# First block of a two-block fp32 network: V and O projections token-major, cross-attention keys and values between the hyena steps, stacked filter matmuls

## Chip, core and metric

One core of one Trainium2 chip runs the whole program in one launch. The metric is the device time of the launch in microseconds, the median of three runs. The engines are TensorE (PE: matmuls; PEld is its loading of weights), VectorE (DVE), ScalarE (ACT), GpSimd (POOL) and SyncE (SP, which issues most DMAs). Tiles have 128 partitions; on chip memory is SBUF, and matmuls write into the eight banks of PSUM, of 128x512 fp32 each.

## The reference

T = 512 tokens, D = 1024, 256 memory tokens, all fp32. `rms` is a norm over the features. Only the first block is touched, and from the second block a table of the decay's rates.

```
u = rms(x, mix_g) @ w_in                       # 1024 -> 1536 (z, g1, g2) + 1024 (q, k) + 512 v + 512 o + 16 gates
hy = conv3(u[:, :1536]);  qk = silu(conv3(u[:, 1536:2560]))
hid  = sin(fr1 * (feat @ w1 + b1)); hid = sin(fr2 * (hid @ w2 + b2))
filt = (hid @ w3) * decay                      # L x (2 orders, 2 directions, 512)
spec = rfft(concat(filt fwd, 0, flip(filt bwd[1:])))
z, g1, g2 = split(hy)
for o, gate in ((0, g1), (1, g2)):             # hyena
    z = gate * (irfft(rfft(z, 2L) * spec[o])[:L] + z * skip[o])
y_hy = group_rms(z, 8 groups)
y_ml = group_rms(sigmoid(o_pre) * (mlstm(q, k, v, gates) + mlstm of the reversed tokens), 4 heads)
h = x + concat(y_hy, y_ml) @ w_out
k_mem, v_mem = rms(mem, mem_g) @ wk, rms(mem, mem_g) @ wv
h = h + softmax(rms(h, x_g) @ wq · k_mem / 16) v_mem @ wo
h = h + square(relu(rms(h, ff_g) @ ff_w1)) @ ff_w2
out = second_block(rms(h, fin_g))              # gated convolution, RG-LRU with rate 8 * softplus(-lam), gated FFN
```

## The kernel before

Every weight comes as a strip of 128x1024 fp32 (512 KB), 302 in all, in a ring of four slots. SP loads strip n + 4 when TensorE has done strip n. ScalarE copies a strip to `w_hi`, rounded to fp32r (`high`; `ahead(n)` does strip n + 3, L882). POOL forms `w_lo = raw - w_hi` in two halves (`low`, L440). Activations are split into `XH` and `XL` in the same way, and each product is three matmuls of 128x128 by 128x512: high by high, low by high, high by low (`three`, L472 to L474). `strip` does 24 of these for one output tile of 128 features by 512 tokens. Activations are thus feature-major, [features, tokens].

Five blocks of code, one for each engine, are written out by hand, and semaphores join them: `lo_ready` (a strip's low half is there), `pe_done` (a strip is used), `evac` (a PSUM bank is read), and many of one stage alone. Each engine runs its instructions in the order of its block; nothing is scheduled by a planner.

The order of strips on TensorE, which is that of all queues:

1. 16 strips of memory's keys (8, with 256 columns) and values (8) against the normed memory `NH`, `NL`. Between them stand the matmuls of the hyena's filter: `feat @ w1`, `hid @ w2` and, at four places (`TAPS_AFTER`), four matmuls `hid @ w3` (L550), from which VectorE makes forward and backward taps, their sum and difference (`sums_and_differences`) and low halves (L1281). VectorE then squares and splits x.
2. Spectrum: 5 strips of cosines and sines against the taps, which ScalarE copies out to `Hc`, `Hs`, `HB`.
3. The norm of x (L500), then 8 strips for V and O, feature-major; VectorE scales each (L1340), TensorE transposes it (`turn`, L575), ScalarE copies it to `VX` or through a sigmoid to `TM`.
4. 8 strips for q and k with VectorE's convolution of three taps; 1 strip of gates; the first 4 of 12 strips for z, g1, g2 (32 of 96 `blocks` of one k tile each), convolved by VectorE (`z_convolved`, L1367 to L1379) and turned (`z_turn`, L575). VectorE computes the gates' cumulative sums between them.
5. The walk: 32 mLSTM steps (4 heads, 2 directions, 4 chunks of 128). In a step TensorE does q·k (L662) and its share of the other 64 blocks of z; `row` (L636) broadcasts a gate row every four steps. VectorE makes the argument `min(row + A, 0)` (`arg`, L1438), ScalarE the exp of it (L1024), VectorE the masked weight (L1447, L1452), and TensorE multiplies it with V (L651).
6. Hyena: for each of the two orders four forward products (`("F", j)`, with `ZH`, `ZL`) and four inverse ones (`("I", j)`, with `QH`, `QL`), two products to a strip, 4 strips an order, in the order `HY_ORDER`. For each j VectorE multiplies with the spectrum (L1572 to L1577) and adds up to `qs` (L1584, L1586), ScalarE makes `QH` (L1060), POOL `QL` (L460; the last one VectorE, L1590). Between the orders VectorE forms the gated z (L1556, L1600 to L1607) and `ZL` (L1524). `back` (L680) turns the mLSTM output, and at the end the hyena output, into the feature-major `XH`, `XL`.
7. 8 strips of w_out, of which the first four begin with the half that takes the mLSTM output. Then queries, attention, its output, the feed-forward in 64 strips. After the norm behind attention (`norm(3)`) VectorE works out softplus(-lam) of the second block in small instructions (L1737 to L1766). Then the second block.

Of the kernel before, what the change touches and what calls it, by code (L numbers as in the profile page):

```python
# [47 lines left out]
N_SPEC, N_VO, N_QK, N_GATE, N_Z, N_HY = 5, 8, 8, 1, 12, 4  # L48
N_KV, N_SQ, N_FF, N_IN, N_MG, N_FFN = 16, 8, 64, 48, 32, 68
S_KV = 0  # L50
S_SPEC = S_KV + N_KV
S_VO = S_SPEC + N_SPEC
S_QK = S_VO + N_VO
S_GATE = S_QK + N_QK
S_Z = S_GATE + N_GATE
S_HY = S_Z + N_Z
S_WOUT = S_HY + 2 * N_HY
# [10 lines left out]
E_SPEC = N_KV  # L68
E_VO = E_SPEC + N_SPEC
E_QK = E_VO + N_VO  # L70
E_GATE = E_QK + N_QK
E_Z = E_GATE + N_GATE
E_HY = E_Z + N_Z
E_WOUT = E_HY + 8
# [9 lines left out]
HY_ORDER = (("F", 0), ("F", 1), ("F", 2), ("I", 0), ("F", 3), ("I", 1), ("I", 2), ("I", 3))  # L84
TAPS_AFTER = (3, 4, 7, 9)
STEPS = 4 * 2 * TT
BLOCKS = N_Z * KT
BLOCKS_FIRST = 4 * KT
# [69 lines left out]
def build(nc, A, out):  # L158
    ctx = ExitStack()
    with ctx:  # L160
# [3 lines left out]
        def sem(name):  # L164
# [50 lines left out]
        memf = at("memf", KT * MEM, 152 * KB)  # L215
        mem_sq = at("mem_sq", KT * MEM, 64 * KB)
        NH = at("NH", KT * MEM, 160 * KB, F32R)
        NL = at("NL", KT * MEM, 168 * KB, F32R)
        K = at("K", KT * MEM, 48 * KB)
        V = at("V", 2 * D, 56 * KB)  # L220
# [47 lines left out]

        def tap(kind, half, k):

            n = (kind * 2 + half) * 2 * TT + k
            return tile(taps[0], n) if n < 28 else tile(taps[(n - 28) // 2 + 1], n % 2)
# [13 lines left out]
        ld_filt = sem("ld_filt")  # L286
        ld_taps = sem("ld_taps")
        ld_x = sem("ld_x")
# [8 lines left out]
        f_mem = sem("f_mem")  # L297
        f_sin = sem("f_sin")
        f_tap = sem("f_tap")
        f_used = sem("f_used")  # L300
# [16 lines left out]
        t_done = sem("t_done")  # L317
# [40 lines left out]
        mem_col = sem("mem_col")  # L358
# [52 lines left out]
        def _(sp):  # L411
# [3 lines left out]
            for n in range(RING):  # L415
                load(n, n)
# [19 lines left out]
        def _(pool):  # L436
# [31 lines left out]
        def _(pe):  # L468
# [1625 lines left out]
```

## Time and profile before

| | |
|---|---|
| time, median of 3 runs | 1871.77 us (1869.42 to 1874.78) |
| the profiled execution's own time | 1876.67 us |
| its span | 1872.8 us |
| TensorE busy | 1751.2 us, 94% of the span |
| VectorE busy | 940.8 us, 50% |
| POOL busy | 820.5 us, 44% |
| ScalarE busy | 633.8 us, 34% |
| moved by DMA | 169.28 MB, mean 90 GB/s |

Busy shares are means over stages with different limits, so the rows below are cut by stage. A duration of a matmul overlaps that of the next; what one costs when nothing waits is the distance between two starts. In brackets behind a row of the timeline stands the idle time of the engine ahead of it and what ended it. The span is 3.9 us shorter than the time of the same execution.

### The profile page before, as it was taken

The numbers are of one execution on the slowest core, as the hardware profiler recorded it, in microseconds if no ns is written. First come the engines' busy times: TensorE is split into PE (matmuls) and PEld (weight loads), VectorE is DVE, ScalarE is ACT, GpSimd is POOL, SyncE is SP. The second block draws the span as 40 slices with busy tenths as digits, with TensorE's granted clock in tenths as the row PEclk, the third lists the DMA queues.
The fourth block names the chain that finished last, engine by engine and source line by source line (L and its number), as shares of the span: only waits on it lengthen the run. The fifth ranks groups of instructions, "written<-read, shape, count | busy, mean of one in ns | idle before, by whom it ended". The sixth has DMA issues, their size and how long they took to land.

```text
span 1872.8 us, 21992 instructions
## 1 busy us (share of the span) xinstructions
PE 1751.2 (94%) x7718; PEld 1422.1 (76%) x7718; DVE 940.8 (50%) x1285; ACT 633.8 (34%) x789; POOL 820.5 (44%) x614
## 2 busy tenths in 40 slices
PE   5889998985899898999999999999999999999996
PEld 4677875763678586888888788888888888888885
DVE  5843287888752448242435666765333443132135
ACT  3322342232242341221213466566333442222222
POOL 3343452124344134444444466565444444444443
PEclk9989998988899999999999999999999999999998
DMA  4232221111222022223222233333322323232232
GB/s 162 90 113 68 90 90 34 46 45 45 90 90 90 13 100 79 93 99 101 90 101 94 98 111 113 101 112 101 101 93 98 101 90 101 90 100 96 95 101 90
DMA packets 47694, 169.28 MB, mean 90 GB/s; under 512 B 5204, under 2 KB 5204, under 8 KB 47320
## 3 DMA queue, kind: packets, MB, share of 16 engines
q1 hardware_dynamic: 44640, 160.45, 25.9%
q10 hardware_dynamic: 3000, 8.09, 1.3%
q8 instruction: 36, 0.59, 0.1%
q14 instruction: 18, 0.15, 0.0%
HBM read 166.43 MB, written 2.10 MB: 90 GB/s over the span
## 4 chain that ended last, share of the span: by engine, by line
PE 42%; issue 20%; POOL 12%; DVE 1%; POOLq 0%; ACT 0%; DVEq 0%
PE ps L472 14%; PE ps L473 14%; PE ps L474 14%; POOL m_w_lo L440 12%; DVE m_h L1951 0%; DVE m_s L1212 0%; PE ps L500 0%; POOL m_QL L460 0%; DVE m_qs L1584 0%; POOLq L448 0%; POOLq L446 0%; DVE m_qs L1586 0%; DVE m_s L1926 0%; DVE m_ftmp L1576 0%; DVE m_ftmp L1574 0%
## 5 line engine op out<-in xcount | busy, mean ns | idle before, releaser
L440 POOL TENSOR_TENSOR m_w_lo<-m_raw,m_w_hi 128x512 fp32r<-128x512 f32 x604 | 806.1, 1356 | 979.6 <-ACT m_w_hi L882 979.4
L882 ACT ACTIVATE m_w_hi<-m_raw 128x1024 fp32r<-128x1024 f32 x302 | 317.7, 1056 | 659.6 <-DMA m_raw<-in_strips 656.5
L472 PE MATMUL ps<-m_XH,m_w_hi 128*128 128x512 f32 x1160 | 466.6, 402 | 0.8 <-POOL m_w_lo L440 0.5
L473 PE MATMUL ps<-m_XL,m_w_hi 128*128 128x512 f32 x1160 | 454.8, 392 | 0.0
L474 PE MATMUL ps<-m_XH,m_w_lo 128*128 128x512 f32 x1160 | 454.7, 392 | 0.0
L472 PEld LDWEIGHTS ps<-m_XH,m_w_hi 128*128 128x128 f32 x1160 | 219.3, 189 | 56.5 <-issue 10.0
L473 PEld LDWEIGHTS ps<-m_XL,m_w_hi 128*128 128x128 f32 x1160 | 219.6, 189 | 46.9 <-issue 2.4
L474 PEld LDWEIGHTS ps<-m_XH,m_w_lo 128*128 128x128 f32 x1160 | 219.7, 189 | 46.6
L472 PE MATMUL ps<-m_FH,m_w_hi 128*128 128x512 f32 x432 | 168.3, 390 | 2.0 <-DVE m_FL L1205 2.0
L474 PE MATMUL ps<-m_FH,m_w_lo 128*128 128x512 f32 x432 | 168.1, 389 | 0.0
L473 PE MATMUL ps<-m_FL,m_w_hi 128*128 128x512 f32 x432 | 168.1, 389 | 0.0
L472 PE MATMUL ps<-m_YH,m_w_hi 128*128 128x512 f32 x384 | 150.9, 393 | 4.9 <-DVE m_s L1776 4.9
L474 PE MATMUL ps<-m_YH,m_w_lo 128*128 128x512 f32 x384 | 150.1, 391 | 0.0
L473 PE MATMUL ps<-m_YL,m_w_hi 128*128 128x512 f32 x384 | 150.0, 391 | 0.0
L472 PEld LDWEIGHTS ps<-m_FH,m_w_hi 128*128 128x128 f32 x432 | 81.1, 188 | 19.6 <-DVE m_FL L1205 2.9
L474 PEld LDWEIGHTS ps<-m_FH,m_w_lo 128*128 128x128 f32 x432 | 81.1, 188 | 17.0
L473 PEld LDWEIGHTS ps<-m_FL,m_w_hi 128*128 128x128 f32 x432 | 81.1, 188 | 16.6
L472 PEld LDWEIGHTS ps<-m_YH,m_w_hi 128*128 128x128 f32 x384 | 72.5, 189 | 20.9 <-issue 5.8
L473 PEld LDWEIGHTS ps<-m_YL,m_w_hi 128*128 128x128 f32 x384 | 72.4, 189 | 15.5 <-issue 0.5
L474 PEld LDWEIGHTS ps<-m_YH,m_w_lo 128*128 128x128 f32 x384 | 72.4, 189 | 15.1
L1791 DVE TENSOR_TENSOR m_h<-m_h,ps 128x512 f32 x24 | 16.5, 687 | 104.9 <-PE ps L474 104.9
L1923 DVE TENSOR_TENSOR m_s<-ps,m_rstd 128x512 f32<-128x512 f32 x22 | 15.2, 691 | 97.1 <-PE ps L474 97.1
(310 smaller groups left out, 2226.2 us busy)
## 6 DMA issues: line engine op xcount, KB each, us to landing
m_raw<-in_strips SPq DMA_DIRECT2D x302, 512.0 KB, 3.2
m_x_in<-in_x ACTq DMA_DIRECT2D x8, 256.0 KB, 4.1
m_x_res<-in_x ACTq DMA_DIRECT2D x1, 2048.0 KB, 7.9
out<-m_h SPq DMA_DIRECT2D x8, 256.0 KB, 2.1
m_memf<-in_mem ACTq DMA_DIRECT2D x1, 1024.0 KB, 11.2
m_decay<-in_decay ACTq DMA_DIRECT2D x1, 1024.0 KB, 16.1
m_w<-in_w ACTq DMA_DIRECT2D x1, 512.0 KB, 14.4
m_skip<-in_skip ACTq DMA_DIRECT2D x1, 512.0 KB, 3.8
```

The source lines that it names most:

```text
L440: nc.gpsimd.tensor_tensor(w_lo[:, c], raw[:, c], f(w_hi[:, c]), ALU.subtract).then_inc(lo_ready, 1)
L472: pe.matmul(dst, w_hi[:, c], xh, start=first, stop=False)
L473: pe.matmul(dst, w_hi[:, c], xl, start=False, stop=False)
L474: return pe.matmul(dst, w_lo[:, c], xh, start=False, stop=last)
L882: act.activation(w_hi[:, c], raw[:, c], ACT.Copy).then_inc(hi_ready, 1)
L1791: dve.tensor_tensor(hm, hm, ps[:, u, :], ALU.add).then_inc(evac, 1)
L1923: dve.tensor_tensor(s0[:], ps[:, u, :], rstd[:], ALU.mult).then_inc(evac, 1)
```

## The change

- **Order of strips.** V and O (8) first, then the spectrum (5), gates (1), q and k (8), z (12); keys and values lie in the hyena part; `S_...` and `E_...` are renumbered.
- **V and O token-major.** `vo_strip` holds the activation still and streams the weights, so that the result is [tokens, features] and needs no turn. Eight PSUM banks gather them over four strips each. The norm's factor is then one for each partition: TensorE sums the squares into a column (`x_cols`), and ScalarE scales as it copies out. For this x is loaded first, by SP, in four pairs of tiles; ScalarE makes `XH`, VectorE `XL` and the sum of squares.
- **Filters.** `hid` holds its 64 rows twice and `hneg` the second copy with the sign turned; `w3` is stacked for K = 128. A `unit` is two matmuls, which give the sum and the difference at once. VectorE needs one operation for the decay and one for the low half; 8 units lie inside V/O strips 3 to 6.
- **Norms in the spectrum stage.** The norms of x (over partitions) and memory stand between the two parts of the first spectrum strip; memory is normalised before its split, so that keys and values are plain copies later. The softplus chain moves here too, from behind `norm(3)`; its results have columns of their own.
- **Gates, then q and k.** VectorE's gate chain lies around the first q/k tile.
- **Walk.** Two strips of z (16 blocks) before it instead of four, 80 blocks inside. ScalarE makes the argument itself, as `Relu(-row - A)` out of PSUM, and exp with scale -1; VectorE's `arg` is gone.
- **Hyena.** Keys in two groups of four strips, values in eight strips behind the second order; ScalarE copies both out. PSUM banks of the forward products are freed one by one (`z_used`). The low halves of the mLSTM output come after the first product on VectorE. The hyena output's low half goes to `YM`, attention's to `OL`.

```diff
-S_KV = 0
-S_SPEC = S_KV + N_KV
...
+S_VO = 0
+S_SPEC = S_VO + N_VO
+S_GATE = S_SPEC + N_SPEC
+S_QK = S_GATE + N_GATE
+S_Z = S_QK + N_QK
 S_HY = S_Z + N_Z
-S_WOUT = S_HY + 2 * N_HY
+S_WOUT = S_HY + 2 * N_HY + N_KV
...
-BLOCKS_FIRST = 4 * KT
+BLOCKS_FIRST = 2 * KT
...
+            sp.dma_start(const[:, 0:NCOL], A["const"][:, 0:NCOL]).then_inc(ld_const, 16)
+            x_pair(0)
+            load(0, 0)
+            x_pair(1)
+            load(1, 1)
+            x_pair(2)
+            x_pair(3)
+            load(2, 2)
+            load(3, 3)
...
+                for part, side in enumerate((hid, hneg)):
+                    mm = pe.matmul(ps[:, b + part, :], side[:, tt * P:(tt + 1) * P], w3[:, o * T:(o + 1) * T],
+                                   start=True, stop=True)
...
+                        pe.matmul(dst, XH[:, a], w_hi[:, c], start=(k == 0), stop=False)
+                        pe.matmul(dst, XL[:, a], w_hi[:, c], start=False, stop=False)
+                        mm = pe.matmul(dst, XH[:, a], w_lo[:, c], start=False, stop=(k == KT - 1))
...
+            for tt in range(TT):
+                mm = pe.matmul(ps[:, 6, tt:tt + 1], acc[:, tt * P:(tt + 1) * P], ones[:, 0:1], start=True, stop=True)
+            mm.then_inc(x_cols, 1)
+            vo_strip(3, {1: 0, 3: 1})
+            vo_strip(4, {2: 2, 3: 3})
+            vo_strip(5, {1: 4, 3: 5})
+            vo_strip(6, {1: 6, 3: 7})
+            vo_strip(7, {})
...
+                    if s == 0 and part == 0:
+                        pe.wait_ge(vo_kept, N_VO)
+                        pe.wait_ge(mem_sum, 1)
+                        pe.matmul(ps[:, 4, 0:MEM], ones, s0[:, 0:MEM], start=True, stop=True).then_inc(norm_all, 1)
+                        pe.matmul(ps[:, 5, :], ones, acc[:], start=True, stop=True).then_inc(norm_all, 1)
...
+            forward(0, 0)
+            forward(0, 1)
+            keys(0)
+            keys(1)
+            pe.wait_ge(y_ready, 1)
+            back(12, 0)
+            keys(2)
+            keys(3)
+            forward(0, 2)
+            forward(0, 3)
+            for j in range(TT):
+                inverse(0, j)
+            for i in range(4, KT):
+                keys(i)
+            pe.wait_ge(z_ready, 4)
+            pe.wait_ge(kv_out, KT)
+            for j in range(TT):
+                forward(1, j)
+            for j in range(TT):
+                inverse(1, j)
+            for i in range(KT):
+                values(i)
...
-                act.activation(e, e, ACT.Exp).then_inc(m_exp, 1)
+                act.activation(e, ps[:, 5, causal(n)], ACT.Relu, bias=misc[:, c:c + 1], scale=-1.0).then_inc(m_arg, 1)
                 act.wait_ge(m_arg, n + 1)
-                e = (s0, s1)[n % 2][:, causal(n)]
-                act.activation(e, e, ACT.Exp).then_inc(m_exp, 1)
+                act.activation(e, e, ACT.Exp, scale=-1.0).then_inc(m_exp, 1)
...
-                dve.tensor_scalar((s0, s1)[n % 2][:, causal(n)], ps[:, 5, causal(n)], misc[:, c:c + 1], 0.0,
-                                  ALU.add, ALU.min).then_inc(m_arg, 1)
...
+    parts = [pairs(w_in[:, 2560:3584]), spec, strips(gates), strips(w_in[:, 1536:2560]), strips(w_in[:, 0:1536]),
+             order[0:1], keys[0:4], order[1:4], keys[4:8], order, pairs(x["xa_wv"]),
+             strips(x["w_out"]), strips(x["xa_wq"]), strips(x["xa_wo"])]
```

What stands in a row on TensorE in the opening, before the change, at the first filter matmuls: keys of memory (`m_NH`, `m_NL`), the turned norm, and four matmuls with `w3`.

```order
L472 MATMUL ps<-m_NH,m_w_hi 128x256
L473 MATMUL ps<-m_NL,m_w_hi 128x256
L474 MATMUL ps<-m_NH,m_w_lo 128x256
L538 MATMUL ps<-m_const,m_rstd 128x1 x2
L550 MATMUL ps<-m_w,m_hid 128x512 x4
L472 MATMUL ps<-m_NH,m_w_hi 128x256
```

And in the changed kernel, at its first filter matmuls, inside V/O strip 3, where weights are streamed against `XH` and `XL`:

```order
L580 MATMUL ps<-m_w_hi,m_XH 128x512
L581 MATMUL ps<-m_w_hi,m_XL 128x512
L582 MATMUL ps<-m_w_lo,m_XH 128x512
L562 MATMUL ps<-m_w,m_hid 128x512
L562 MATMUL ps<-m_w,m_hneg 128x512
L580 MATMUL ps<-m_w_hi,m_XH 128x512
```

Memory's keys have left the opening, and a group of filter matmuls has two in place of four.

VectorE in the walk, before: a z tile's convolution ends (L1371 to L1379), then argument (L1438), mask (L1447) and weight (L1452) of the steps.

```order
L1371 SCALAR_TENSOR_TENSOR m_cbuf<-m_pbuf,m_const,m_ctmp 128x512
L1377 SCALAR_TENSOR_TENSOR m_cbuf<-m_pbuf,m_const,m_cbuf 128x256
L1379 SCALAR_TENSOR_TENSOR m_cbuf<-m_pbuf,m_const,m_cbuf 128x256
L1438 TENSOR_SCALAR m_s<-ps,m_misc 128x128
L1447 TENSOR_TENSOR m_s<-m_s,m_const 128x128
L1452 SCALAR_TENSOR_TENSOR m_W<-ps,m_s 128x256
L1438 TENSOR_SCALAR m_s<-ps,m_misc 128x128
L1447 TENSOR_TENSOR m_s<-m_s,m_const 128x128
```

After, at the same kind of place:

```order
L1640 SCALAR_TENSOR_TENSOR m_cbuf<-m_pbuf,m_const,m_ctmp 128x512
L1646 SCALAR_TENSOR_TENSOR m_cbuf<-m_pbuf,m_const,m_cbuf 128x256
L1648 SCALAR_TENSOR_TENSOR m_cbuf<-m_pbuf,m_const,m_cbuf 128x256
L1665 TENSOR_TENSOR m_s<-m_s,m_const 128x128
L1670 SCALAR_TENSOR_TENSOR m_W<-ps,m_s 128x384
L1665 TENSOR_TENSOR m_s<-m_s,m_const 128x128
L1670 SCALAR_TENSOR_TENSOR m_W<-ps,m_s 128x512
```

The argument has left VectorE's row, which has two instructions a step instead of three.

POOL in the first order of the hyena, before: low halves of weights (`m_w_lo`) and of the spectral products (`m_QL`) in separate runs.

```order
L440 TENSOR_TENSOR m_w_lo<-m_raw,m_w_hi 128x512 x4
L460 TENSOR_TENSOR m_QL<-m_qs,m_QH 128x1024 x3
L446 UNCONDITIONAL_BRANCH
L440 TENSOR_TENSOR m_w_lo<-m_raw,m_w_hi 128x512 x8
L446 REGISTER_ALU
L446 COMPARE_AND_BRANCH
L460 TENSOR_TENSOR m_QL<-m_qs,m_QH 128x1024 x3
```

After, in the first order:

```order
L478 TENSOR_TENSOR m_w_lo<-m_raw,m_w_hi 128x512 x2
L484 REGISTER_ALU
L484 COMPARE_AND_BRANCH
L496 TENSOR_TENSOR m_QL<-m_qs,m_QH 128x1024
L478 TENSOR_TENSOR m_w_lo<-m_raw,m_w_hi 128x512 x4
L496 TENSOR_TENSOR m_QL<-m_qs,m_QH 128x1024 x2
```

Two strips' low halves now stand between the first product's low half and the other two.

## Rows read from the trace of the kernel before

**Rows 1.** Windows: length, busy us (count) of PE, PEld, DVE, ACT, POOL; clock, DMA, GB/s.

```profile
0.00:113.29 113.29, 79.66 (x440) 64.66 (x441) 66.05 (x97) 34.36 (x41) 47.22 (x40) 0.94 0.36 121
113.29:165.32 52.03, 50.85 (x217) 41.60 (x217) 24.72 (x33) 15.72 (x24) 17.08 (x13) 0.97 0.26 86
165.32:213.63 48.31, 47.96 (x222) 39.17 (x222) 10.10 (x12) 12.55 (x16) 18.09 (x15) 1.00 0.27 87
213.63:299.93 86.30, 77.96 (x346) 62.80 (x346) 61.16 (x66) 31.96 (x35) 38.45 (x26) 0.95 0.26 86
299.93:411.57 111.64, 102.20 (x467) 76.70 (x466) 90.79 (x202) 31.55 (x74) 23.06 (x18) 0.92 0.11 38
...
415.67:524.55 108.88, 73.78 (x272) 57.11 (x273) 86.74 (x121) 28.55 (x44) 39.85 (x24) 0.80 0.17 60
524.55:1872.80 1348.25, 1318.79 (x5758) 1080.06 (x5756) 597.17 (x750) 475.72 (x555) 636.77 (x480) 0.99 0.29 95
```

**Rows 2.** Timeline of TensorE: start us, us, line, operation, tiles, form, [idle before].

```profile
40.14 0.28 PE L472 MATMUL ps<-m_NH,m_w_hi 128*128 128x256 f32 x1
40.26 0.28 PE L473 MATMUL ps<-m_NL,m_w_hi 128*128 128x256 f32 x1
...
44.05 3.67 PE L550 MATMUL ps<-m_w,m_hid 64*128 64x512 f32 x8 [0.34 <-DVE m_misc L1311]
...
505.38 0.63 PE L472 MATMUL ps<-m_XH,m_w_hi 128*128 128x512 f32 x1
...
714.07 0.47 PE L472 MATMUL ps<-m_YH,m_w_hi 128*128 128x512 f32 x1 [4.91 <-DVE m_s L1776]
...
902.79 0.39 PE L472 MATMUL ps<-m_YH,m_w_hi 128*128 128x512 f32 x1
903.02 0.39 PE L473 MATMUL ps<-m_YL,m_w_hi 128*128 128x512 f32 x1
```

**Rows 3.** TensorE's waits, 0 to 430 us: line, releaser, us in total, times, longest.

```profile
PE ps L521 <- POOL m_w_lo L440: 9.7, 2, 7.6
PE ps L575 <- DVE m_cbuf L1379: 8.7, 3, 6.4
PE ps L636 <- DVE m_s L1438: 8.5, 7, 1.7
```

**Rows 4.** TensorE's waits, 415 to 525 us.

```profile
PE ps L472 <- DVE m_ZL L1524: 21.3, 2, 17.2
PE ps L472 <- DVE m_QL L1590: 4.5, 2, 2.8
PE ps L472 <- DVE m_ftmp L1576: 4.0, 1, 4.0
```

**Rows 5.** Busy time of a piece of 20 us, columns as in rows 1.

```profile
460.00:480.00 20.00, 7.78 (x27) 6.08 (x28) 17.60 (x25) 2.11 (x2) 2.17 (x2) 0.61 0.00 0
```

**Rows 6.** POOL's timeline, first low halves.

```profile
6.82 2.48 POOL L440 TENSOR_TENSOR m_w_lo<-m_raw,m_w_hi 128x512 fp32r<-128x512 f32 x2 [6.37 <-ACT m_w_hi L882]
```

**Rows 7.** VectorE's timeline, first instruction of the softplus chain.

```profile
697.61 0.17 DVE L1737 SCALAR_TENSOR_TENSOR m_misc<-m_const 128x8 f32<-128x8 f32 x1 [0.70 <-ACT m_rstd L898]
```

**Rows 8.** Groups by line in the walk: count, busy us, mean ns, idle before.

```profile
L1438 DVE TENSOR_SCALAR m_s<-ps,m_misc 128x512 f32<-128x512 f32 (+3 forms) x32 | 17.5, 549 | 6.5 <-PE ps L636 5.8
...
L882 ACT ACTIVATE m_w_hi<-m_raw 128x1024 fp32r<-128x1024 f32 x9 | 9.4, 1055 | 22.6 <-DMA m_raw<-in_strips 22.6
```

**Rows 9.** Groups by line and form in the hyena part; last L1584 alone, ns min/median/max.

```profile
L440 POOL TENSOR_TENSOR m_w_lo<-m_raw,m_w_hi 128x512 fp32r<-128x512 f32 x18 | 25.6, 1447 | 22.5 <-ACT m_w_hi L882 22.5
...
L1584 DVE TENSOR_TENSOR m_qs<-m_s,m_s 128x512 f32<-128x512 f32 x8 | 10.2, 1274 | 0.8
...
L1556 DVE TENSOR_TENSOR m_TM<-m_TM,m_skip 128x512 f32<-128x512 f32 x8 | 9.2, 1209 | 0.1
...
L1586 DVE TENSOR_TENSOR m_qs<-m_ftmp 128x512 f32<-128x512 f32 x8 | 7.5, 936 | 0.3
...
L1584 DVE TENSOR_TENSOR m_qs<-m_s,m_s x8: 693/1474/1530, 432.5 to 494.5; 128x512 f32<-128x512 f32 x8
```

More of the change, by code:

```diff
@@ L267, in tile, with tap_pair @@
             return buf[:, k * T:(k + 1) * T]
+        def tap_pair(half, k):
+            n = k * 2 + half
+            at0 = (0, 4, 10, 14, 15, 16)
+            home = next(i for i in range(5) if n < at0[i + 1])
+            return taps[home][:, (n - at0[home]) * 2 * T:(n - at0[home] + 1) * 2 * T]
         def tap(kind, half, k):
-            n = (kind * 2 + half) * 2 * TT + k
-            return tile(taps[0], n) if n < 28 else tile(taps[(n - 28) // 2 + 1], n % 2)
+            return tap_pair(half, k)[:, kind * T:(kind + 1) * T]
         def dtile(buf, k):
@@ new lines, in forward @@
+            def forward(o, j):
+                n = HY_STRIPS[o][j // 2]
+                pe.wait_ge(lo_ready, (n + 1) * 2)
+                for part in range(2):
+                    i = 2 * j + part
+                    if o:
+                        b, used = i % 4, 8 + i - 3 if i >= 4 else None
+                    else:
+                        b, used = (0, 1, 2, 5, 0, 1, 2, 0)[i], {4: 1, 5: 2, 6: 3, 7: 5}.get(i)
+                    if used is not None:
+                        pe.wait_ge(z_used, used)
+                    half = (part + j // 2) % 2
+                    for k in range(2):
+                        mm = three(ps[:, b, :], n % RING, (j % 2) * 4 + part * 2 + k,
+                                   tile(ZH, k * 2 + half), tile(ZL, k * 2 + half), k == 0, k == 1)
+                    mm.then_inc(pe_done if part and j % 2 else freq, 1)
@@ new lines, in inverse @@
+            def inverse(o, j):
+                n = HY_STRIPS[o][2 + j // 2]
+                pe.wait_ge(lo_ready, (n + 1) * 2)
+                if j < TT - 1:
+                    pe.wait_ge(p_ready, o * (TT - 1) + j + 1)
+                else:
+                    pe.wait_ge(p_last, o + 1)
+                if j == 0:
+                    pe.wait_ge(mixed, 4)
+                    if o:
+                        pe.wait_ge(i_used, TT)
+                    else:
+                        pe.wait_ge(kv_out, 4)
+                for part in range(2):
+                    half = (part + j // 2) % 2
+                    for k in range(2):
+                        mm = three(ps[:, 4 + half * 2 + k, :], n % RING, (j % 2) * 4 + part * 2 + k,
+                                   tile(QH, 2 * j + part), tile(QL, 2 * j + part), j == 0, j == 3)
+                if j % 2:
+                    mm.then_inc(pe_done, 1)
@@ L956, in _, with spectrum @@
-            act.wait_ge(f_pair, 2 * TT)
-            for k in range(KT):
-                act.dma_start(tile(x_in, k), A["x"][k]).then_inc(ld_x, 16)
-            for s in range(N_SPEC):
+            def spectrum(s):
                 ahead(S_SPEC + s)
@@ L2008, in strips, with pairs @@
         return s
+    def pairs(w):
+        halves = [w[:, c:c + T] for c in (0, T)]
+        return np.stack([np.concatenate([s[2 * i * P:(2 * i + 1) * P], s[(2 * i + 1) * P:(2 * i + 2) * P]], axis=1)
+                         for s in halves for i in range(4)])
     w_in = x["w_in"]
```

977 lines of the change are left out of this document (524 added, 453 removed), and 2 rows, old and new, of the table COLUMNS.

## The prediction

> **What bounds the kernel now.** I read the table of stretches first [rows 1]. From 524.55 us to the end TensorE is busy 1318.79 of 1348.25 us at a granted clock of 0.99: almost nothing is to be had there, and the change touches little of it. The 524.55 us ahead hold 433 us of busy time at clocks of 0.80 to 1.00, so this is where it can gain. The matmuls themselves cost what their pitch says [rows 2]: a 128x512 one starts 0.23 us after the last (902.79, 903.02; over a strip 0.2267), so a strip of 24 takes 5.44 us; a 128x256 one 0.12 us. The waits come next [rows 3, 4]. In the opening 9.7 us for POOL's low halves (7.6 in one piece). Then 8.7 for the convolved tiles that are turned (6.4 in one piece, ahead of the walk), 8.5 in the walk for the exp arguments that VectorE makes. In the hyena part: 21.3 for `ZL` (17.2 of it in one piece, between the two orders), 4.5 for `QL`, 4.0 for the products. There the stretch of 108.88 us holds 192 matmuls of the hyena and 48 of w_out, 240 x 0.2267 = 54.4 us; the rest are waits (17.2 + 4.5 + 4.0 and smaller ones), transposes and the lower clock that stands behind the waits (20 us with 7.78 us of TensorE at a clock of 0.61) [rows 5].
>
> **The change, stage by stage, on TensorE.**
>
> *Opening to the first spectrum matmul, 113.3 us now.* Sixteen strips of memory's keys and values leave it, the eight V and O strips enter it (48.3 us of their own now, 165.32 to 213.63 [rows 1], which go). Summed up anew: the first weights. Now the first low halves are written from 6.82 to 9.30 [rows 6]; behind the constants, a 512 KB pair of x and two scaled copies on ScalarE I take 12 (9.3 if x costs nothing, 16 if each of the three stands in line). Eight strips, 43.5. The filter matmuls: now 3.67 us for the four of 128x512 in plain fp32 at one place, which the row counts as 8 [rows 2], 0.9 each; the change has 16 of them, 14.5, and 0.9 for the second hidden layer. Half clock in the first strip, 4.5, as the first matmuls ran now. Waits for the sum of squares of x before the columns' norm (VectorE adds 2048, 1024 and 512 wide behind ScalarE's last square) about 4.1, and 0.5 at the last unit's low half (a strip lies between the last unit and the spectrum). Sum 80; bounds 74 (no waits, x for nothing) to 92 (the strips late behind x, and the 9.7 us wait for low halves back).
>
> *Spectrum, 52.0 us now:* the two norms bring matmuls of 1.7 us, and the one for memory needs ScalarE's square and VectorE's reduction of eight tiles, behind the last unit: 3.8. The softplus chain goes in here on VectorE; now it starts at 697.61 and the tile behind it reaches TensorE at 714.07 [rows 2, 7], so it is under 16.5 us, beside a stretch where VectorE is busy 24.72 of 52.03 [rows 1], so it hides, at most against the next stage's first convolution. Less a wait of 1 us for ScalarE's copies at its end, which the gate strip now covers: 56.5 (52 to 60).
>
> *Gate, QK, two Z strips, 86.3 us now for 13 strips:* nine strips 49.0, two 10.9, the gate's turns and row 3.7 as now, 64 (61 to 70). The waits for the turned tiles, 8.3 of the 8.7 us, go, for the gate chain on VectorE now has eight strips to run beside; what is late next is the last QK convolution, inside the 64.
>
> *The walk, 111.6 us now.* Sixteen more blocks of three matmuls each: 48 x 0.2267 = 10.9, and two more turns of four transposes, 0.8. ScalarE takes over the 32 argument steps, which VectorE did in 17.5 us out of a busy 90.79 of 111.64 [rows 1, 8], so that VectorE's period is shorter and part of the 8.5 us wait goes; but VectorE gets two more convolutions (3.1 us each), and ScalarE's first step now stands in line behind its strip copies, which waited 22.6 us for DMA [rows 8]. I take 116 (107 if all 8.5 us and most of the lower clock go, 123 if nothing goes). Then the 4.1 us for `ZL` [rows 4] as now.
>
> *Hyena.* Added: keys, 8 x 24 x 0.12 = 23.0, values, 8 x 12 x 0.2267 = 21.8, in all 44.8. Half of the keys lie between the second and third forward product (now 4.0 us of wait [rows 4] and the turns of the mLSTM output), half in the 17.2 us gap. So the first order stays 56.6 us (415.67 to 472.22), with 0.7 of spill. The values lie behind the last inverse product, over VectorE's norm of the hyena output, which now only the first halves of w_out cover: 19.2 us from 505.38 [rows 2] to 524.55, 10.9 of it matmuls. This becomes 21.8 + 10.9 + 4.3 of turns = 37.0. The price is on POOL: 24 strips' low halves of 2 x 1.45 us fall into the stretch for 9 now [rows 9], 70 us for 26. VectorE's operations with two SBUF inputs take 0.69 us at the fastest and 1.47 to 1.53 at the median and the most; I read the difference as POOL's doing [rows 9]. Over the three lines of them with the most, 24 operations, that makes 26.9 us against 16.6, a loss of 10.3 with POOL busy 39.85 of 108.88 us, 0.37 [rows 1]; with 70 + 14 of 135, 0.61, it becomes 17 by the share and 22 by POOL's time, say 19, so 9 more, of which I put 7.5 on the path: 4.5 in the first order and 3 in the second. Sum 56.6 + 0.7 + 4.5 + 33.2 + 3 + 37.0 = 135 (127 if POOL costs nothing and the clock comes back, 162 as in the first rival). The second halves of w_out begin at 80 + 56.5 + 64 + 116 + 4.1 + 135 = 455.6 instead of 524.55: -69.
>
> *Behind it:* the softplus chain no longer stands between norm and the first hidden tile; its share of the wait of 4.9 us at 714.07 [rows 2] goes, -5. The rest is the same work.
>
> The Trainium skill has a rule that speaks against this: SBUF — State Buffer, section "SBUF: two separate sides", calls the pair of ports that VectorE and GpSimd share an exclusive lock held for a whole instruction, so that the loser waits in full. The row of L1584 agrees in kind (0.69 against 1.47 to 1.53 us). By its strictest reading every one of the 48 operations of this kind that meets a POOL instruction loses a whole one: 48 x 0.37 x 1.45 = 26 us now, where the rows show 10, and 48 x 0.61 x 1.45 = 42 in the changed kernel. The step of 16 in place of my 9 would make 1805; I stay with the measured durations.
>
> **Sum.** -69 - 5 = -74 against the profiled execution's own 1876.67 us (1872.8 of span and 3.9 around it): 1802.7. The median of the runs shown, 1871.77, lies 4.9 lower, so 1798.
>
> **Rivals.**
> - *A: the hyena part has no room.* The keys and values do not fall into the gaps, since the waits are VectorE's and slide along with what is put before them. Then 108.9 + 44.8 + 8 of contention = 161.7, 27 more than I sum: 1825. For it: the clock of 0.80, and POOL's load. Against it: the 17.2 us gap is one piece, with DMA and POOL idle.
> - *B: the opening slips.* ScalarE works in order: x's copies, two sines, four squares, the strips' copies. If a strip waits behind them as TensorE now waits 7.6 us for one [rows 3], and x comes later: +12, 1810.
> - *C: the walk goes by ScalarE.* Its copies wait for strips (22.6 us [rows 8]) in the same line as the argument and the exp; all of it on the path gives +22.6: 1821. Against it: ScalarE has only 31.55 of 111.64 us busy.
> - *D: better.* No further contention in the hyena part (-8), and the walk's clock from 0.92 to 1.0 (-9): 1781.
> - *E: slower.* The matmuls of the hyena stretch, 54.4 + 44.8 = 99.2 us at full clock, all run at half of it, as in the row of 0.61 [rows 5]. Some 16 us of that are in the sum already, 83 come on top: 9 more than the gain, 1881. It decides from about nine tenths of the stretch at the lower level, against a mean of 0.80 over the stretch now [rows 1]; the added work makes TensorE's idle pieces shorter, which speaks against it.
>
> **Chances.** Forecast (1786 to 1812) 0.60, A 0.10, B 0.09, C 0.08, D 0.11, E 0.02. The range has to hold 8 in 10: from D less 6 us to A plus 3, 1775 to 1828; it leaves out E and the tails of A, C and D in sum, and takes in the bounds of opening, walk and hyena one at a time. A measurement of this kernel tells 0.3%, 5.6 us, from no change: faster by more 0.97, within 0.01, slower 0.02.
>
> **What would show it.** First spectrum matmul near 80 us, not over 92; the memory norm's wait under 5 us in the spectrum; the walk's start near 201 and its length under 123; no wait of 17 us for `ZL` between the orders, but one of a few us behind the fourth of the second set of keys; the eight sums that L1584 makes at 1.3 to 1.6 us in most cases; values directly behind the last inverse product and no wait for the normed output; second halves of w_out near 456; no wait at the first hidden tile. Wrong it is if the stretch of hyena and values is over 150 us (A), if ScalarE's line is the releaser of TensorE's waits in the walk (C), or if the part from w_out on is longer than now by more than 5 us, which no term here foresees.

## The result, and the profile after

The changed kernel takes 1809.53 us (median of 4 runs, 1807.44 to 1812.86), the kernel before 1870.7 beside it: ratio 0.9675, 95% interval 0.9663 to 0.9688. Five more runs later gave 1804.97 (1802.48 to 1809.42), ratio 0.9656 (0.9638 to 0.9674). The forecast was 1798, with a range of 1775 to 1828. The profiled execution has a span of 1805.6 us where that of before had 1872.8.

The stretches of the changed kernel, cut at the same events as in [rows 1]: first spectrum matmul, first gate matmul, first matmul of the walk, its last turn, first forward product, second halves of w_out. Columns as there.

```profile
0.00:80.28 80.28, 65.70 (x237) 45.87 (x237) 44.09 (x45) 38.28 (x44) 33.20 (x26) 0.98 0.38 139
80.28:134.24 53.96, 51.24 (x221) 41.25 (x220) 22.26 (x49) 23.99 (x39) 12.96 (x10) 1.00 0.15 49
134.24:203.39 69.15, 64.93 (x287) 51.96 (x285) 54.92 (x58) 25.70 (x29) 35.09 (x24) 0.98 0.27 87
203.39:321.73 118.34, 113.21 (x523) 85.14 (x522) 80.92 (x180) 50.63 (x109) 26.58 (x20) 0.93 0.14 48
321.73:325.83 4.10, 0.00 (x1) 0.00 (x0) 4.07 (x6) 3.42 (x4) 0.00 (x0) 0.68 0.32 102
325.83:462.10 136.27, 117.24 (x560) 96.14 (x561) 104.19 (x125) 50.52 (x74) 90.82 (x56) 0.91 0.33 109
462.10:1805.60 1343.50, 1320.62 (x5758) 1077.43 (x5756) 585.01 (x718) 471.77 (x548) 638.73 (x480) 1.00 0.29 96
```

| stretch, us | before | my sum | after |
|---|---|---|---|
| opening | 113.29 | 80 | 80.28 |
| spectrum | 52.03 | 56.5 | 53.96 |
| V and O alone | 48.31 | 0 | 0 |
| gates, q and k, z ahead of the walk | 86.30 | 64 | 69.15 |
| walk | 111.64 | 116 | 118.34 |
| wait for `ZL` | 4.10 | 4.1 | 4.10 |
| hyena, values, first halves of w_out | 108.88 | 135 | 136.27 |
| all the rest | 1348.25 | 1343.25 | 1343.50 |

TensorE was idle for 92.1 of the first 524.55 us before (its busy times add up to 432.4) and is for 49.8 of the first 462.1 us now. So two thirds of the 62.45 us are waits that are gone; I put the rest down to fewer turns and a higher clock (the hyena stretch has 0.91 where it had 0.80), which no run measures apart. Nor does a run undo the order of strips or the token-major V and O alone: what they bring is read from the stretches.

TensorE's waits over the whole span of the changed kernel (line, releaser, total, times, longest), the counterpart of [rows 3, 4]:

```profile
PE ps L517 <- DVE m_ZL L1737: 9.3, 2, 5.2
PE ps L580 <- POOL m_w_lo L478: 7.7, 3, 5.6
...
PE ps L517 <- DVE m_QL L1808: 4.4, 2, 2.7
PE ps L681 <- ACT m_s L1198: 4.2, 2, 2.2
PE ps L517 <- POOL m_w_lo L478: 4.0, 2, 3.7
PE ps L517 <- POOL m_QL L496: 2.9, 3, 2.3
...
PE ps L622 <- DVE m_s L1517: 2.7, 1, 2.7
```

The 17.2 us ahead of the second order are 5.2. Two waits are new and were in no term: 4.2 us for ScalarE's argument in the walk, and 3.7 us for a low half among the q and k strips. The experiments start from these. On TensorE's timeline they stand here, with the gap between the orders:

```profile
165.76 0.50 PE L517 MATMUL ps<-m_XH,m_w_hi 128*128 128x512 f32 x1 [3.67 <-POOL m_w_lo L478]
...
240.96 0.91 PE L681 MATMUL ps<-m_gM,m_sel 4*128 4x512 f32 x1 [2.22 <-ACT m_s L1198]
...
390.79 0.80 PE L517 MATMUL ps<-m_ZH,m_w_hi 128*128 128x512 f32 x1 [5.20 <-DVE m_ZL L1737]
```

### The profile page after: what moved, and what is told of

The parts are those of the page before. It is cut to its first block, busy times and chain, and to the rows that moved or that the text cites. A ratio compares the mean times of both kernels' runs of the same rounds, so it can differ in the third digit from the quotient of the medians.

```text
span 1805.6 us, 21590 instructions
## 1 busy us (share of the span) xinstructions
PE 1732.9 (96%) x7580; PEld 1397.8 (77%) x7580; DVE 895.5 (50%) x1179; ACT 664.3 (37%) x846; POOL 837.4 (46%) x614
## 4 chain that ended last, share of the span: by engine, by line
PE 37%; issue 23%; POOL 17%; DVE 1%; POOLq 0%; ACT 0%; DVEq 0%
POOL m_w_lo L478 17%; PE ps L517 12%; PE ps L519 12%; PE ps L518 12%; POOL m_QL L496 0%; DVE m_h L2132 0%; DVE m_s L1429 0%; POOLq L486 0%; POOLq L484 0%; PE ps L545 0%; DVE m_s L2107 0%; ACT m_QH L1243 0%; DVE m_acc L1876 0%; DVE m_qs L1802 0%; DVE m_s L1427 0%
## 5 line engine op out<-in xcount | busy, mean ns | idle before, releaser
L478 POOL TENSOR_TENSOR m_w_lo<-m_raw,m_w_hi 128x512 fp32r<-128x512 f32 x604 | 822.6, 1384 | 931.3 <-ACT m_w_hi L998 931.2
L517 PE MATMUL ps<-m_XH,m_w_hi 128*128 128x512 f32 x1096 | 440.1, 402 | 4.4 <-POOL m_w_lo L478 4.0
L519 PE MATMUL ps<-m_XH,m_w_lo 128*128 128x512 f32 x1096 | 430.0, 392 | 0.0
L518 PE MATMUL ps<-m_XL,m_w_hi 128*128 128x512 f32 x1000 | 392.6, 393 | 0.0
L517 PEld LDWEIGHTS ps<-m_XH,m_w_hi 128*128 128x128 f32 x1096 | 207.6, 189 | 57.6 <-issue 8.8
L519 PEld LDWEIGHTS ps<-m_XH,m_w_lo 128*128 128x128 f32 x1096 | 207.5, 189 | 44.0
L518 PEld LDWEIGHTS ps<-m_XL,m_w_hi 128*128 128x128 f32 x1000 | 189.8, 190 | 40.7 <-issue 2.0
```

Of the source, the lines that this page charges most:

```text
L478: nc.gpsimd.tensor_tensor(w_lo[:, c], raw[:, c], f(w_hi[:, c]), ALU.subtract).then_inc(lo_ready, 1)
L517: pe.matmul(dst, w_hi[:, c], xh, start=first, stop=False)
L518: pe.matmul(dst, w_hi[:, c], xl, start=False, stop=False)
L519: return pe.matmul(dst, w_lo[:, c], xh, start=False, stop=last)
```

## The experiments

Stretches below are named by their ends: "walk" runs from its first matmul to the first forward product, so that it has the 4.1 us for `ZL` in it (122.44 us in the changed kernel, 122.07 in `again`). Each has its own medians and its own profile; the same kernel's medians lay 4.6 us apart in two sets (1809.53 and 1804.97), so I read medians for what is over 5 us, and stretches of the profile for less. A stretch whose code is the same in two runs need not have the same length either: the walk took 117.5 to 122.4 us in six profiles that leave it as it is (the last section has the rows). A price that goes by one pair of profiles is therefore given as a range where such profiles allow one.

**again: the changed kernel once more.** No edit.

> The changed kernel as it is, beside the three below on the same chip: the value that they are compared with. 1809.5 measured so far; my sum took the profiled execution's excess of 4.9 us over the median as a constant, and if it is only this execution's own, the profile of this run and its median will not be 4.9 us apart either.

Measured: 1804.97 us, and the profiled execution is the median one. That of the first set lay 2.1 us under its median (1807.44 to 1809.53), that of before 4.9 over. So the 4.9 us is an execution's own excess and no constant of the program. Where it lay in the profile of before isn't known; terms summed anew from counts don't contain it, and to take the whole of it off the forecast had no ground.

**keys_cut: do the keys lie in gaps?**

```diff
-                for k in range(KT):
+                for k in (0, KT - 1):
                     c = slice(k * MEM, (k + 1) * MEM)
                     mm = three(ps[:, K_BANKS[i], 0:MEM], n % RING, k, NH[:, c], NL[:, c],
```

> The changed kernel with a quarter of the key matmuls: 6 of 24 in each of the 8 strips, so the keys are wrong sums; strips are still loaded, split and waited for. 144 matmuls of 0.12 us, 17.3 us of TensorE's work, are gone. If the keys lie in gaps (my sum): the gap in front of the second order opens again to some 14 us, the first group hardly counts, and the time falls by 1 to 5 us. Rival A (the waits slide along, the keys come on top): it falls by 15 to 17 us, to about 1793.

Measured: 1807.99 us (1805.15 to 1810.98). From the first forward product to the first values' matmul, the changed kernel and then keys_cut:

```profile
325.83:423.16 97.33, 81.14 (x401) 67.86 (x402) 81.64 (x95) 33.70 (x48) 65.50 (x38) 0.87 0.29 96
```

```profile
321.03:418.24 97.21, 64.05 (x257) 50.60 (x257) 84.47 (x95) 33.20 (x48) 65.24 (x38) 0.81 0.27 95
```

TensorE has 144 matmuls and 17.1 us of busy time less, and the stretch is 0.1 us shorter. The time became waiting: two gaps of 7.79 and 8.50 us stand ahead of the second order, where the changed kernel has one of 5.20. So what comes from VectorE's chain and the copies behind it sets the length; the keys cost nothing there. Rival A is out for the keys. The values, which stand in no gap, were in my sum at their full 21.8 us.

**pool_light: what does POOL's work cost VectorE?**

```diff
+                    if n in K_STRIPS or n in V_STRIPS:
+                        for part in range(2):
+                            c = slice(n % RING * STRIP + part * (STRIP // 2), n % RING * STRIP + part * (STRIP // 2) + 8)
+                            nc.gpsimd.tensor_tensor(w_lo[:, c], raw[:, c], f(w_hi[:, c]), ALU.subtract).then_inc(lo_ready, 1)
...
-                        mm = pe.matmul(ps[:, b + mt, :], NH[:, a], w_lo[:, c], start=False, stop=(k == KT - 1))
+                        mm = pe.matmul(ps[:, b + mt, :], NH[:, a], w_hi[:, c], start=False, stop=(k == KT - 1))
```

> The changed kernel in which POOL writes only 8 columns of the low halves of the 16 strips of keys and values; TensorE multiplies the high halves in their place, so it has the same number of matmuls, and keys and values lack their low products. What is measured is the price of POOL's extra work in the hyena stretch of 136.3 us. My sum: 7.5 us of contention on the path, so about 1802, with the two-input sums of VectorE back near the 26.9 us of before (24 operations; 32.5 in the changed kernel). Rival, the exclusive lock by its strictest reading: 15 us or more, under 1795. Rival: the path there is TensorE's, and the time stays within 1 us.

Measured: 1799.06 us (1798.42 to 1803.12). The same stretch, and the one of the values and w_out's first halves behind it (39.24 us in the changed kernel):

```profile
327.09:417.43 90.34, 77.47 (x400) 65.53 (x401) 73.00 (x95) 33.84 (x48) 42.25 (x38) 0.92 0.31 105
417.43:454.14 36.71, 35.11 (x163) 28.88 (x161) 16.58 (x30) 17.16 (x26) 13.36 (x18) 1.00 0.43 149
```

The three lines of VectorE's sums in the hyena part (count, busy us, mean ns), first in the changed kernel, then in pool_light:

```profile
L1771 DVE TENSOR_TENSOR m_TM<-m_TM,m_skip 128x512 f32<-128x512 f32 x8 | 12.3, 1598 | 0.1
L1802 DVE TENSOR_TENSOR m_qs<-m_ftmp 128x512 f32<-128x512 f32 x8 | 11.5, 1438 | 0.3
L1800 DVE TENSOR_TENSOR m_qs<-m_s,m_s 128x512 f32<-128x512 f32 x8 | 8.7, 1090 | 0.8
```

```profile
L1820 DVE TENSOR_TENSOR m_qs<-m_s,m_s 128x512 f32<-128x512 f32 x8 | 11.0, 1373 | 0.8
...
L1791 DVE TENSOR_TENSOR m_TM<-m_TM,m_skip 128x512 f32<-128x512 f32 x8 | 8.3, 1092 | 0.1
...
L1822 DVE TENSOR_TENSOR m_qs<-m_ftmp 128x512 f32<-128x512 f32 x8 | 6.7, 832 | 0.3
```

32.5 us against 26.0 (26.9 before), and the whole is 7.0 + 2.5 = 9.5 us shorter. VectorE's busy time in the first stretch falls by 8.6 us (81.64 to 73.00) with the same 95 instructions, so the low halves cost time through VectorE. One of the three lines went the other way (`m_s,m_s`: 8.7 to 11.0), for a reason that the timeline gives. In the changed kernel, VectorE and then POOL:

```profile
355.31 0.69 DVE L1800 TENSOR_TENSOR m_qs<-m_s,m_s 128x512 f32<-128x512 f32 x1
356.03 2.78 DVE L1802 TENSOR_TENSOR m_qs<-m_ftmp 128x512 f32<-128x512 f32 x1
...
360.65 0.68 DVE L1792 TENSOR_TENSOR m_ftmp<-ps,m_Hc 128x512 f32<-128x512 f32 x1
361.42 1.51 DVE L1800 TENSOR_TENSOR m_qs<-m_s,m_s 128x512 f32<-128x512 f32 x1
```

```profile
355.40 2.87 POOL L496 TENSOR_TENSOR m_QL<-m_qs,m_QH 128x1024 fp32r<-128x1024 f32 x1
359.98 2.40 POOL L496 TENSOR_TENSOR m_QL<-m_qs,m_QH 128x1024 fp32r<-128x1024 f32 x1 [1.72 <-ACT m_QH L1243]
```

POOL's two instructions end at 358.27 and 362.38, the sums that began beside them at 358.81 and 362.93: each 0.55 us behind. All 16 of the 24 sums here that are slow, the 12 of before and the 9 of pool_light end 0.54 to 0.55 us after the POOL instruction that was under way when they began; those that met none take 0.68 to 0.69. So a sum loses about what is left of POOL's instruction, be it a half or `QL`, and which line pays is a matter of when it starts. An operation with one input in PSUM loses nothing (L1792, 0.68 us beside the second `QL`). This agrees with the exclusive lock of the Trainium skill (SBUF — State Buffer, "SBUF: two separate sides"). My strictest reading took a whole instruction of POOL for each meeting, a step of 16 us; the losses of the three lines are 10.3 us before, 15.9 here and 9.4 in pool_light.

The 9.5 us rest on one pair of profiles. The first stretch took 94.9 to 98.7 us in eleven profiles that leave its code alone, so the added low halves cost 7 to 11 us on the path, and my 7.5 is inside. What I had not summed is their share behind the inverse products, the 2.5.

**chain_back: the softplus chain behind the norm again.** VectorE's 28 instructions and ScalarE's exp move back to where the kernel before had them.

```diff
+            norm(3)
+            lam = const[:, COL["lam"]:COL["lam"] + 8]
+            m = [misc[:, 8 * i:8 * i + 8] for i in range(8)]
...
+            dve.sem_inc(gain_two, 1)
```

> The changed kernel with the softplus chain back behind the norm after attention (VectorE) and its exp back on ScalarE there. My sum gave this move 5 us: the time goes from 1809.5 to about 1814.5, the wait ahead of the first hidden matmul is back at 4.9 us, and the spectrum stage (53.96 us) stays within 0.5 us of itself. Rival: that wait belongs to the norm and not to the chain, and then the time stays within 1 us.

Measured: 1815.64 us (1812.98 to 1821.18), 6 us over the first set of the changed kernel and 11 over the second. The row of [rows 2] at the first hidden matmul is back:

```profile
PE ps L517 <- DVE m_s L1958: 4.4, 1, 4.4
```

From the second halves of w_out to the end:

```profile
458.28:1811.20 1352.92, 1324.23 (x5757) 1079.46 (x5755) 594.50 (x746) 474.61 (x551) 637.24 (x480) 0.99 0.28 95
```

That is 6 to 10 us more than the 1343.2 to 1346.8 of the other profiles, so the 5 us is there and was on the low side; what comes on top of the wait of 4.4 is open. The spectrum stage was 55.56 us here with the chain gone from it and 53.96 with it, and keys_cut, which has the chain in it, also took 55.56, so the chain is hidden there.

**qk_ahead: a copy ahead of the gates' wait.** ScalarE's timeline of the changed kernel shows why a low half came late at 165.76. The exp of the gates' rows waits 6.92 us for VectorE's sums, and the copy of the strip that TensorE needs next stands behind it:

```profile
160.45 1.06 ACT L1167 ACTIVATE m_gE<-m_gE 4x1024 f32<-4x1024 f32 x1 [6.92 <-DVE m_gE L1627]
161.41 1.04 ACT L998 ACTIVATE m_w_hi<-m_raw 128x1024 fp32r<-128x1024 f32 x1
```

```diff
             ahead(S_QK)
+            ahead(S_QK + 1)
             act.wait_ge(g_rows, 1)
             act.activation(gE[0:4, :], gE[0:4, :], ACT.Exp, scale=-1.0).then_inc(g_em, 1)
             for u in range(1, N_QK):
-                ahead(S_QK + u)
+                if u < N_QK - 1:
+                    ahead(S_QK + u + 1)
                 silu(u)
```

> The changed kernel with ScalarE's copies for the q and k strips one step earlier: the copy of the strip three ahead no longer stands behind the wait for the gates' rows (VectorE's sums), which ended at 160.4 us with 6.92 us of waiting. If the 3.67 us that TensorE waited at 165.76 us, which no term of my sum had, come from that order, they go: the stage of gates, q and k and two z strips falls from 69.15 to about 65 us and the time from 1809.5 to about 1805.5. Rival: the strip's DMA or POOL is what is late, and the wait stays or comes one strip later.

Measured: 1801.68 us (1798.24 to 1803.34). The stage:

```profile
133.71:197.45 63.74, 63.33 (x287) 50.80 (x285) 52.35 (x58) 25.84 (x29) 37.72 (x24) 1.00 0.29 94
```

69.15 becomes 63.74, 5.4 us: the wait of 3.7, and the lower clock behind it (the stage's clock goes from 0.98 to 1.00). The stage took 69.1 to 69.2 us in all seven profiles that leave its code alone, and 63.7 to 63.8 in this one, combo, combo_arg and combo_open. My sum had said 64.

**walk_late: ScalarE's copies one step later in the walk.** On ScalarE's timeline the argument of a step stands behind a copy that waits for its strip, and TensorE's row at 240.96 behind that argument:

```profile
239.60 1.06 ACT L998 ACTIVATE m_w_hi<-m_raw 128x1024 fp32r<-128x1024 f32 x1 [3.66 <-DMA m_raw<-in_strips]
240.56 0.35 ACT L1198 ACTIVATE m_s<-ps,m_misc 128x128 f32<-128x128 f32 x1
```

```diff
-                    if m > 2 and first_step(m * KT + 1) == n - 1:
+                    if m > 2 and first_step(m * KT + 1) == n - 2:
                         ahead(S_Z + m)
-                    if m < N_Z - 2 and first_step(m * KT + 16) == n - 1:
+                    if m < N_Z - 2 and first_step(m * KT + 16) == n - 2:
                         keep(m)
```

> The changed kernel with ScalarE's strip copies and copies of turned z tiles one walk step later, so that ScalarE does not wait for the DMA (30.0 us in ten waits in the walk) ahead of the step's argument. If rival C is what the two waits of TensorE (4.2 us for the argument, each with some 4 us of lower clock behind it) come from, they go and the walk falls from 118.3 to 110 to 113 us, the time to 1801 to 1804. Rival: the walk goes by TensorE's own work and VectorE's chain, and the time stays within 2 us.

Measured: 1801.63 us (1799.91 to 1803.22). The walk in the changed kernel, and then in walk_late:

```profile
203.39:325.83 122.44, 113.21 (x523) 85.14 (x522) 84.98 (x185) 54.05 (x113) 26.58 (x20) 0.92 0.15 50
```

```profile
205.42:317.86 112.44, 106.74 (x524) 81.15 (x523) 84.68 (x185) 53.73 (x113) 26.72 (x20) 0.98 0.16 54
```

ScalarE's waits for DMA in it, before the edit and behind it:

```profile
ACT m_w_hi L998 <- DMA m_raw<-in_strips: 30.0, 10, 3.7
```

```profile
ACT m_w_hi L998 <- DMA m_raw<-in_strips: 14.3, 6, 3.5
```

10.0 us go, of which only 4.2 were the waits of TensorE's row; the rest is clock (0.92 to 0.98). But in keys_cut, with the old order and the same waits, the walk was 117.47 us at a clock of 0.97:

```profile
PE ps L681 <- ACT m_s L1198: 4.1, 2, 2.1
```

Against that profile 5.0 us go. So this order is worth 5 to 10 us (walk_late, combo and combo_open all have 112.4 to 112.5), and the time fell by 3.3 to 7.9. Rival C's mechanism was there, at a quarter to half of its price.

**arg_dve and combo_arg: what the argument's move is worth.** Both put VectorE's `arg` back and take ScalarE's Relu out; combo_arg does so on top of combo (below).

```diff
+            arg(0)
             for n in range(STEPS):
+                if n + 1 < STEPS:
+                    if n:
+                        dve.wait_ge(m_w, n)
+                    arg(n + 1)
                 weigh(n)
...
-                act.activation(e, ps[:, 5, causal(n)], ACT.Relu, bias=misc[:, c:c + 1], scale=-1.0).then_inc(m_arg, 1)
                 act.wait_ge(m_arg, n + 1)
-                act.activation(e, e, ACT.Exp, scale=-1.0).then_inc(m_exp, 1)
+                act.activation(e, e, ACT.Exp).then_inc(m_exp, 1)
```

> The changed kernel with the argument of the exp back on VectorE, as the kernel before had it, and still 80 blocks in the walk. My sum let the argument's move to ScalarE win most of the 8.5 us that TensorE waited for it: then the walk grows from 118.3 to 122 to 127 us and the time is 1813 to 1818. Rival: the walk of 118.3 us goes by TensorE's blocks and the waits only change their owner, and then the time stays within 2 us.

> combo (1793.2) with the argument of the exp back on VectorE. In the changed kernel that undo did not cost anything (the walk 121.7 us from its first matmul to the first of the hyena, against 122.4). If ScalarE's wait for DMA hid the worth of the move, then it shows here, where that wait is gone: the walk grows from 112.5 to 116 to 120 us, the time to 1797 to 1801. Rival: the move is worth nothing, within 2 us.

Measured: arg_dve 1806.94 us (1805.84 to 1813.26), combo_arg 1801.76 (1798.44 to 1803.78). Their walks:

```profile
205.25:326.91 121.66, 109.02 (x524) 82.11 (x523) 100.95 (x217) 37.85 (x81) 27.13 (x20) 0.96 0.15 50
```

```profile
195.16:316.88 121.72, 108.86 (x523) 82.15 (x522) 102.74 (x217) 37.48 (x81) 27.50 (x20) 0.97 0.15 49
```

With ScalarE's copies in their old place the move is worth little or nothing (122.44 against 121.66; against the shortest walk of that order, 117.47, it is 4.2). TensorE's wait for the argument only changes its owner: 4.2 us for ScalarE in the changed kernel, 4.6 for VectorE in arg_dve. With the copies one step later the move is worth 9.2 us (112.48 against 121.72), more than the 3.5 to 7.5 that I expected. The change took the work off the engine that was late and put it behind another queue's wait.

**blocks32 and combo_b32: is it the same whether z's blocks lie ahead of the walk or in it?**

```diff
-BLOCKS_FIRST = 2 * KT
+BLOCKS_FIRST = 4 * KT
...
             z_convolved(0)
+            z_convolved(1)
+            z_convolved(2)
```

> The changed kernel with 32 z blocks ahead of the walk and 64 in it, as the kernel before had it. My sum held this part to be neutral: 10.9 us of matmuls and two turns leave the walk and come ahead of it. If so the walk shrinks by 10 to 12 us, the stage ahead grows by as much, and the time stays within 2 us of 1809.5. Rival: the walk is held by VectorE and ScalarE, so the 16 blocks were free inside it, and the time rises by 5 to 11 us.

> combo with 32 blocks ahead of the walk instead of 16. In the changed kernel that took 5 us off the time (11.8 us more ahead, 20.0 less in the walk). If the 8 us over were ScalarE's DMA waits ahead of the argument, fewer strips in the walk only meant fewer of them, and with walk_late's order it is neutral now: within 2 us of combo. Rival: blocks in the walk cost more than outside whatever ScalarE does, and it is 4 to 8 us faster than combo.

Measured: blocks32 1804.14 us (1802.36 to 1806.28), combo_b32 1792.34 (1788.17 to 1797.09). The stage ahead of the walk and the walk, of blocks32 and then of combo_b32:

```profile
136.13:217.08 80.95, 76.71 (x344) 61.74 (x342) 60.87 (x68) 27.37 (x31) 37.83 (x26) 0.98 0.27 87
217.08:319.55 102.47, 94.95 (x467) 71.57 (x467) 78.92 (x175) 51.89 (x111) 23.79 (x18) 0.98 0.15 49
```

```profile
129.86:205.42 75.56, 75.19 (x343) 60.62 (x342) 58.27 (x68) 27.50 (x31) 40.12 (x26) 1.00 0.29 94
205.42:306.02 100.60, 94.91 (x467) 71.71 (x466) 79.58 (x175) 52.48 (x111) 23.56 (x18) 0.97 0.15 50
```

Both stages together: 191.59 us in the changed kernel, 183.42 in blocks32; 176.22 in combo, 176.16 in combo_b32. So the move is neutral in itself, as I summed. In the changed kernel it cost 8.2 us by this pair, and 3.2 with the walk of keys_cut (69.15 and 117.47) in place of 122.44; TensorE's wait for the argument is 0.7 us in blocks32. That each strip more in the walk brings a copy that waits ahead of an argument fits both, but no run shows which copy it is.

**combo: three orders of ScalarE's at once.** qk_ahead, walk_late, and the square of memory ahead of O's sigmoid copies:

```diff
             ahead(7)
+            act.wait_ge(ld_mem, 16)
+            act.activation(mem_sq[:], memf[:], ACT.Square).then_inc(mem_sqr, 1)
             act.wait_ge(pe_done, S_VO + 8)
```

> The changed kernel with three changes of order on ScalarE at once: the copies of qk_ahead, those of walk_late, and the square of memory ahead of the sigmoid copies of O, so that TensorE no longer waits 2.72 us for memory's sum in the spectrum. If the waits are independent: 3.7 + 2.7 + up to 8, so 1795 to 1803. If each waits' end only uncovers the next, 1806 or more.

Measured: 1793.18 us (1789.52 to 1796.53), ratio to the kernel before 0.9581 (0.9561 to 0.9602). Spectrum, gates with q, k and z, walk:

```profile
82.44:133.44 51.00, 51.00 (x222) 41.30 (x221) 22.29 (x49) 23.32 (x39) 13.01 (x10) 1.00 0.16 52
133.44:197.18 63.74, 63.31 (x287) 50.80 (x285) 52.36 (x58) 25.81 (x29) 37.88 (x24) 1.00 0.29 95
197.18:309.66 112.48, 105.46 (x523) 79.98 (x522) 84.94 (x185) 53.65 (x113) 26.66 (x20) 0.99 0.16 54
```

3.0, 5.4 and 10.0 us, 18.4 in all, and they add up; the opening was 2.2 us longer in this execution. This version beats both kernels.

**combo_open: two strips ahead of x.**

```diff
-            x_pair(0)
             load(0, 0)
-            x_pair(1)
+            x_pair(0)
             load(1, 1)
+            x_pair(1)
...
-            act.wait_ge(ld_const, 16)
-            x_highs(0)
             high(0, 0, 1)
-            x_highs(1)
+            act.wait_ge(ld_const, 16)
+            x_highs(0)
             high(1, 1, 1)
+            x_highs(1)
```

> combo with the first two strips of weights loaded ahead of x's first pairs, and ScalarE copying a strip ahead of x's tiles. TensorE waits until 12.4 us for the first low half, 5.6 to 6.5 us behind the first filter matmul. If that low half is what the start hangs on, the first V matmul comes some 2.5 us earlier and the time falls by 1 to 3 us. Rival: x's low half or the second strip's comes later by as much, and nothing changes.

Measured: 1792.95 us (1790.98 to 1794.29), ratio to the kernel before 0.9583, no difference from combo (0.9581). TensorE's first V matmul, in combo and then in combo_open:

```profile
12.60 0.79 PE L580 MATMUL ps<-m_w_hi,m_XH 128*128 128x512 f32 x1 [6.48 <-POOL m_w_lo L478]
```

```profile
11.81 0.76 PE L580 MATMUL ps<-m_w_hi,m_XH 128*128 128x512 f32 x1 [5.09 <-DVE m_XL L1473]
```

The low half of the strip is in time, and x's own low half is late in its place. The start moved by 0.8 us, which is no more than it differs between profiles that leave it alone (11.8 to 12.6).

## Why the prediction was right, and where not

- **Opening** (80, measured 80.28). The first low half came at 12.4 us, where I had 12. The hit to 0.3 us is luck in part: the wait for x's sum was 2.0 us and not 4.1, two later low halves cost 2.1 that I did not have, and the same opening took 78.9 to 82.3 us in the other profiles.
- **Spectrum** (56.5, measured 53.96). Memory's sum cost a wait of 2.7 us and not 3.8, and the clock was 1.00 where before had 0.97, which no term had. The softplus chain hides, and chain_back finds its 5 us behind the norm, and more.
- **Gates, q and k, z** (64, measured 69.15). The failed step is "the gate chain on VectorE now has eight strips to run beside; what is late next is the last QK convolution". I asked what waits for VectorE's sums on TensorE and found room; on ScalarE the exp that waits for them has strip copies behind it. The work itself was right: with the copy moved the stage is 63.74.
- **Walk** (116, measured 118.34). The sum was near, for a reason that was not mine. The blocks and turns cost what I said (combo_b32: 11.8 us more ahead, 11.9 less in the walk). I took 7 us off for the argument's move and the clock behind it, and the move gave 4.2 at most, since ScalarE's copies ahead of it wait for DMA. Yet with the argument on VectorE (arg_dve) the walk without its last 4.1 us is 117.6, not the 123 of my sum; what made the difference is open. By the sign that I set, ScalarE as the releaser of TensorE's waits, rival C holds; I priced it at 22.6 us, the whole wait, and it is 5 to 10.
- **Hyena** (135, measured 136.27). The keys are free, by keys_cut. Up to the first values' matmul I had 98.0 us and it took 97.33; values and first halves took 38.9 where I had 37.0, since I had put no contention there. Half of the sums of L1584 (now L1800), four of eight, were slow, and not most; of L1586 (now L1802) it was five.
- **The base.** I took the profiled execution's 4.9 us over the median off the result. `again` shows that such a difference belongs to one execution, so that the 1802.7 us ahead of this step was the better forecast.

In numbers: the span fell by 67.2 us, and I had 74. The stretches give 6.5 of the 6.8 us between (gates 5.2, walk 2.3, hyena 1.3, spectrum -2.5, opening 0.3), and the rest of the program 0.25. What else separates 1809.5 from 1798 is the 4.9 and the 2.1 by which the new profile lies under its median, less 2.0 for a shorter time around the span.

## What to carry to other kernels

When a step moves to another engine, or a wait is added to one, list what stands behind it in that engine's own order. Both new waits of TensorE here came from work on ScalarE that stood behind a wait that had nothing to do with it, and both went with a change of order on ScalarE alone. Matmuls put into a gap that another engine's chain sets are free, but what feeds them is not: the low halves on POOL slowed that chain and what follows it by 7 to 11 us.

## What the runs showed of the hardware

- A short wait of TensorE costs more than itself: 3.7 us of wait went with 5.4 of stage (clock 0.98 against 1.00), and two waits of 4.2 in all with 5.0 or with 10.0 (0.97 or 0.92 against 0.98).
- One and the same code of a stage has more than one length. The walk of the changed kernel, untouched in keys_cut, took 117.47 us there at a clock of 0.97, and 122.44 at 0.92 in the changed kernel itself, with the same waits for the argument (4.1 and 4.2 us). again had 122.07, pool_light 121.66, qk_ahead 120.91, chain_back 117.66. The row of keys_cut:

```profile
203.56:321.03 117.47, 108.45 (x523) 82.33 (x522) 86.54 (x185) 54.32 (x113) 27.09 (x20) 0.97 0.15 52
```

The spectrum, too, took 53.93 to 53.98 us in seven of these profiles and 55.56 in two, chain_back and keys_cut. The part behind w_out's first halves took 1343.2 to 1346.8 us without the chain in it. The cause stays open; it bounds what one profile says of a stage, to some 5 us in the walk.
- A VectorE sum of two SBUF inputs that begins beside a POOL instruction ends 0.54 to 0.55 us after it (37 of 37 slow ones in three profiles). The most that one lost is thus the rest of a `QL` and not of a half: L1802 has a longest of 2.78 us against 0.69 at the least, and that one began beside `QL` (2.87 us). Its row (ns at least, median, most):

```profile
L1802 DVE TENSOR_TENSOR m_qs<-m_ftmp x8: 691/1661/2778, 338.1 to 416.1; 128x512 f32<-128x512 f32 x8
```
